# Softmax attention's denominators: ones as the stationary operand, and VectorE's 32x32 transposes in place of TensorE's

## What is computed

```python
sc = jnp.einsum("bqgrd,bkgd->bgrqk", qi, k).astype(jnp.float32) * scale
p = jax.nn.softmax(sc, axis=-1).astype(v.dtype)
return jnp.einsum("bgrqk,bkgd->bqgrd", p, v)
```

## Time and profile before

| | us |
|---|---|
| median of three runs | 1561.52 |
| profiled execution, device time | 1560.5 |
| its span | 1558.7 |
| TensorE busy | 1528.3 (98%) |
| VectorE busy | 1139.1 (73%) |
| ScalarE busy | 834.7 (54%) |
| GpSimd busy | 907.3 (58%) |

### The profile page before, as it was taken

The page is one execution under the profiler, slowest core; times in us unless marked ns, Lnnn a source line. Parts: engine busy times, 40 slices in busy tenths (PEclk is TensorE's granted clock), DMA queues, the critical chain, the costliest instruction groups (busy, mean ns, idle before and its releaser), DMA issues.

```text
span 1558.7 us, 23051 instructions
## 1 busy us (share of the span) xinstructions
PE 1528.3 (98%) x7975; PEld 1235.0 (79%) x7975; DVE 1139.1 (73%) x1590; ACT 834.7 (54%) x1552; POOL 907.3 (58%) x644
## 2 busy tenths in 40 slices
PE   7999999999999999999999999999999999999998
PEld 4778888888878766687777888888888888888887
DVE  4799888888739888488459878877768895567542
ACT  4775765766633587423344444444458665454442
POOL 0556765766655876556846767776753467532314
PEclk9999999999999999999999999999999999999999
DMA  8434434434332300276622333333422334322212
GB/s 328 133 122 129 128 108 130 131 107 129 115 94 70 81 28 1 83 239 249 214 67 83 96 92 103 108 109 109 113 83 81 95 102 122 94 62 69 68 41 82
DMA packets 77485, 171.34 MB, mean 110 GB/s; under 512 B 8321, under 2 KB 10753, under 8 KB 73921
## 3 DMA queue, kind: packets, MB, share of 16 engines
q1 hardware_dynamic: 70064, 133.09, 28.7%
q10 hardware_dynamic: 7312, 36.83, 6.7%
HBM read 167.67 MB, written 2.23 MB: 109 GB/s over the span
## 4 chain that ended last, share of the span: by engine, by line
PE 64%; DVE 13%; issue 8%; POOL 6%; DMA 2%; ACT 2%; ACTq 0%; DVEq 0%; POOLq 0%; SPq 0%
PE bank L1401 8%; PE bank L1403 7%; PE bank L1402 7%; PE bank L1419 7%; PE bank L1422 7%; PE bank L1420 7%; POOL w_lo L716 6%; PE bank L1864 4%; DMA w_raw<-ws 2%; PE bank L1866 2%; DVE ada_acc L2155 2%; PE bank L1757 2%; DVE rstd L2454 2%; PE bank L2021 1%; PE bank L1695 1%
## 5 line engine op out<-in xcount | busy, mean ns | idle before, releaser
L716 POOL TENSOR_TENSOR w_lo<-w_raw,w_hi 128x512 fp32r<-128x512 f32 x440 | 644.8, 1489 | 403.2 <-ACT w_hi L775 402.8
L775 ACT ACTIVATE w_hi<-w_raw 128x512 fp32r<-128x512 f32 x444 | 260.4, 624 | 124.0 <-DMA w_raw<-ws 104.2
L1401 PE MATMUL bank<-a_hi_and_lo,w_hi 128*128 128x512 f32 (+1 forms) x800 | 315.8, 395 | 2.4 <-ACT gates_early L840 1.2
L1403 PE MATMUL bank<-a_hi_and_lo,w_lo 128*128 128x512 f32 (+1 forms) x800 | 308.7, 386 | 0.0
L1402 PE MATMUL bank<-a_hi_and_lo,w_hi 128*128 128x512 f32 (+1 forms) x800 | 308.3, 385 | 0.0
L1419 PE MATMUL bank<-b_hi,w_hi 128*128 128x512 f32 x536 | 210.2, 392 | 2.6 <-ACT tmp L1119 1.4
L1422 PE MATMUL bank<-b_lo,w_hi 128*128 128x512 f32 x536 | 209.2, 390 | 0.0
L1420 PE MATMUL bank<-b_hi,w_lo 128*128 128x512 f32 x536 | 209.0, 390 | 0.0
L1401 PEld LDWEIGHTS bank<-a_hi_and_lo,w_hi 128*128 128x128 f32 x800 | 150.4, 188 | 36.6 <-issue 4.4
L1402 PEld LDWEIGHTS bank<-a_hi_and_lo,w_hi 128*128 128x128 f32 x800 | 150.5, 188 | 30.8 <-issue 1.9
L1403 PEld LDWEIGHTS bank<-a_hi_and_lo,w_lo 128*128 128x128 f32 x800 | 150.3, 188 | 30.8
(11 more groups left out here) (447 smaller groups left out, 3183.2 us busy)
## 6 DMA issues: line engine op xcount, KB each, us to landing
w_raw<-ws SPq DMA_DIRECT2D x457, 256.0 KB, 2.7
cs_rows<-cs_scratch ACTq DMA_DIRECT2D x16, 1024.0 KB, 5.2
ada_piece<-ada ACTq DMA_DIRECT2D x16, 1024.0 KB, 5.3
ada_piece<-ada SPq DMA_DIRECT2D x8, 1024.0 KB, 17.6
x_stream<-x SPq DMA_DIRECT2D x2, 1024.0 KB, 8.5
x_stream<-x ACTq DMA_DIRECT2D x1, 2048.0 KB, 7.8
out<-x_stream SPq DMA_DIRECT2D x4, 256.0 KB, 3.3
out<-x_stream SPq DMA_DIRECT2D x8, 128.0 KB, 1.8
```

The costliest lines, as they stand in the source:

```text
L716: nc.gpsimd.tensor_tensor(wlo[b][:, :], full[:, :], r32(whi[b][:, :]), ALU.subtract)\
L775: A(whi[n % RING][:, :], full[:, :], ACT.Copy).then_inc(hi_done, 1)
L1401: mm(out, lh, rh, start=first, stop=False)
L1403: return mm(out, ll, rh, start=False, stop=last)
```

## The change

`take_sums` now makes two matmuls for a pair instead of eight: 64 columns of ones are the stationary operand and the whole `sq[hh]` the moving one, and head 0's sums land on partitions 0 to 63, head 1's on 64 to 127, each repeated over 64 partitions, with the queries in the free dimension. Both stand behind `row_of_max`. VectorE transposes this bank in 32x32 blocks to t[4], inverts one column of each block (16 columns), and transposes these, each repeated 32 times, back to t[5], which has the layout that `scale_pair` multiplies with. `sums_to_columns` stands behind the first maximum of an odd head, `invert_sums` behind the second. `spread_inverse` and `keep_inverse` of ScalarE and `turn_inverse` of TensorE are gone.

```diff
@@ -579,8 +580,8 @@
 
         slab_used, FILLED = fills, N_KV
-        chunks_added, sums_taken, sums_inverted, inverse_turned = exp_masked, st_done, rec_done, xt_done
-        inverse_kept, q_high, inverse_spread = x_kept, e_ready, xs_sc
+        chunks_added, sums_taken = exp_masked, st_done
+        q_high, sums_copied = e_ready, xs_sc
         ADDED_AT, SCANNED = 2 * PAIRS, PAIRS
 
...
@@ -993,19 +994,6 @@
 
-            def spread_inverse(u):
-                act.wait_ge(sums_inverted, SCANNED + u + 1)
-                if u >= 2:
-                    act.wait_ge(o_ev, u - 1)
-                else:
-                    act.wait_ge(yz_ready, PAIRS)
-                A(t[4 + u % 2][:, :].rearrange("p (i d) -> p i d", d=HD),
-                  inv_sum[:, :, None].broadcast_to([P, 2 * NCH, HD]), ACT.Copy).then_inc(inverse_spread, 1)
-
-            def keep_inverse(u):
-                act.wait_ge(inverse_turned, SCANNED + u + 1)
-                A(t[4 + u % 2][:, :], SUMS[:, :], ACT.Copy).then_inc(inverse_kept, 1)
-
             def query_high(h):
...
@@ -1758,25 +1740,16 @@
                 ins.then_inc(pv_done, 1)
 
-            def take_sums(u, hh):
-                pe.wait_ge(chunks_added, ADDED_AT + (NCH - 1) * (2 * u + hh + 1))
+            def take_sums(u):
+                pe.wait_ge(chunks_added, ADDED_AT + (NCH - 1) * (2 * u + 2))
                 if u:
-                    pe.wait_ge(inverse_kept, SCANNED + u)
+                    pe.wait_ge(sums_copied, SCANNED + u)
                 else:
                     pe.wait_ge(qk_std, len(QK))
-                for i in range(NCH):
-                    ins = mm(SUMS[:, (2 * i + hh) * HD:(2 * i + hh + 1) * HD], sq[hh][:, i * P:(i + 1) * P], ones[:, 0:HD], start=True, stop=True)
-                ins.then_inc(sums_taken, 1)
-
-            def last_sums():
                 for hh in range(2):
-                    take_sums(QT - 1, hh)
-
-            def turn_inverse(u):
-                pe.wait_ge(inverse_spread, SCANNED + u + 1)
-                for i in range(NCH):
-                    ins = nc.tensor.transpose(SUMS[:, i * P:(i + 1) * P], t[4 + u % 2][:, i * P:(i + 1) * P], ident)
-                ins.then_inc(inverse_turned, 1)
+                    rows_of = slice(hh * HD, (hh + 1) * HD)
+                    ins = mm(SUMS[rows_of, :], ones[:, rows_of], sq[hh][:, :], start=True, stop=True)
+                ins.then_inc(sums_taken, 2)
 
             def middle_of(n):
...
@@ -1819,26 +1792,20 @@
                 chunks_of(h, 0, NCH)
                 if h % 2 == 0:
-                    take_sums(u - 1, 0)
                     row_of_max(h + 1)
-                    take_sums(u - 1, 1)
+                    take_sums(u - 1)
                     continue
                 if u == 0:
...
                 for c in range(NCH):
                     values(u, c)
-                    if c == 1:
-                        if h + 1 < N_Q:
-                            row_of_max(h + 1)
-                        if u:
-                            turn_inverse(u - 1)
+                    if c == 1 and h + 1 < N_Q:
+                        row_of_max(h + 1)
             for m in range(KT):
                 if m >= N_EARLY:
                     feature_tile(("ga", m), in_a, in_a_lo)
-                feature_tile(("gs", m), in_a, in_a_lo, mid=None if m else last_sums)
-                if m == 0:
-                    turn_inverse(QT - 1)
+                feature_tile(("gs", m), in_a, in_a_lo, mid=None if m else lambda: take_sums(QT - 1))
                 feature_tile(("wa", m), in_b, in_b_lo, (rdyB, PAIRS))
                 if m == KT - 3:
...
@@ -2501,16 +2468,23 @@
                 V.tensor_tensor(qL[b][0:HD, :], qF[own, u, :], r32(qHH[b][own, :]), ALU.subtract).then_inc(q_ready, 1)
 
+            def columns_of(wide):
+                return wide[:, :].rearrange("p (b c) -> p b c", c=SQUARE)
+
+            def sums_to_columns(u):
+                ve.wait_ge(sums_taken, SCANNED + 2 * (u + 1))
+                V.transpose(t[4][:, :], SUMS[:, :]).then_inc(sums_copied, 1)
+
             def invert_sums(u):
-                ve.wait_ge(sums_taken, SCANNED + 2 * (u + 1))
-                if u:
-                    ve.wait_ge(inverse_spread, SCANNED + u)
-                V.reciprocal(inv_sum, SUMS[:, :].rearrange("p (i d) -> p i d", d=HD)[:, :, 0]).then_inc(sums_inverted, 1)
+                ve.wait_ge(sums_copied, SCANNED + u + 1)
+                v(V.reciprocal(inv_sum, columns_of(t[4])[:, :, 0]))
+                v.settle()
+                v(V.transpose(columns_of(t[5]), inv_sum[:, :, None].broadcast_to([P, SEQ // SQUARE, SQUARE])))
 
             def scale_pair(u):
                 ve.wait_ge(pv_done, NCH * (u + 1))
-                ve.wait_ge(inverse_kept, SCANNED + u + 1)
-                V.tensor_tensor(OQ[u % 2][:, :], OQ[u % 2][:, :], t[4 + u % 2][:, :], ALU.mult).then_inc(o_ev, 1)
+                v.settle()
+                V.tensor_tensor(OQ[u % 2][:, :], OQ[u % 2][:, :], t[5][:, :], ALU.mult).then_inc(o_ev, 1)
 
             def split_pair(u):
...
@@ -2541,10 +2515,15 @@
             for h in range(N_Q):
-                if h + 1 < N_Q:
-                    for i in range(NCH):
+                u = h // 2
+                turned = h % 2 and u
+                for i in range(NCH):
+                    if h + 1 < N_Q:
                         max_of(h + 1, i)
-                u = h // 2
+                    if turned and i == 0:
+                        sums_to_columns(u - 1)
+                    if turned and i == 1:
+                        invert_sums(u - 1)
                 if h in (1, 3):
...
@@ -2563,9 +2542,8 @@
                     if u >= 2:
                         split_pair(u - 2)
-                    if u:
-                        invert_sums(u - 1)
             split_pair(QT - 2)
+            sums_to_columns(QT - 1)
             invert_sums(QT - 1)
             scale_pair(QT - 1)
```

More of the change, by code:

```diff
@@ L282 @@
     SUM_AT[_name] = _s
+SQUARE = 32
 ADA_W = 2 * D_MODEL
@@ L405, in build @@
         mx = [maxima[:, 0:NCH], maxima[:, NCH:2 * NCH]]
-        inv_sum = small[:, 312:320]
+        inv_sum = cwh[:, 128:144]
         with Arena():
@@ L1038, in _ @@
                     continue
-                if u:
-                    spread_inverse(u - 1)
-                else:
+                if u == 0:
                     query_high(3)
@@ L1046, in _ @@
                     max_row(h + 1)
-                if u:
-                    keep_inverse(u - 1)
                 if h + 4 < N_Q:
@@ L1051, in _ @@
             round_pair(QT - 2)
-            spread_inverse(QT - 1)
-            keep_inverse(QT - 1)
             round_pair(QT - 1)
```

## The result

The changed kernel takes 1567.78 us, the median of six runs (1564.13 to 1570.84), the one before 1561.80 on the same chips: a ratio of 1.0039, 95% interval 1.0028 to 1.0049. That is 6.0 us slower, where 3.7 were forecast; the value lies in the range that was stated, 1559.3 to 1570.5. The profiled execution is the fastest of the six, 1564.13 us with a span of 1562.3, 3.6 us over the span before.

What follows compares the result with a forecast made beforehand. TensorE, busy 98% of the span, was taken as the bound, with waits for VectorE's maxima opening in its queue. Losses of 5.45 us less 1.75 at the end gave +3.7 us: median 1565.2 us, range 1559.3 to 1570.5.

Steps and rivals of the forecast that it cites:

- rival 2: VectorE's transposes are cheap or hidden in its slack: -2 to +3 us, 1559.5 to 1564.6; chance 33%.
- Prices: Costs per pair: new sums 1.0 us on TensorE; on VectorE transposes 0.69 and 0.74, reciprocal 0.26.
- Rivals 3 and 4: Transposes at half rate, about 1.1 us each: 1570, 12%; sums not side by side: 1572, 3%.
- Even head, +0.25: Even head to next odd: TensorE idles some 0.9 us before the row of maxima, sums follow it; 0.25 us longer.
- Plain odd head, +0.1: Odd to even head, heads 11 and 13: maxima 0.5 us later eat the 0.44 us saved; 0.1 us longer.
- Heads 3 and 7, +0.5 with the even part: VectorE reaches the even head's maxima 1.6 us later, past its 1.14 us idle; +0.5 us each.
- the even part: The step from an even head to the next odd one, forecast 0.25 us longer, included in each pair's sum.
- Head 5, +1.8: Pair with a query tile's rotation on VectorE: 1.6 us fully on the path, 1.8 with the even part.
- head 9, +1.5: Pair with a query tile's rotation: loss as in head 5, less some 0.35 us from leaving GpSimd's adds; 1.5 us.
- it bounds the pair already, and the 1.6 us go fully onto the path: Heads 5 and 9: VectorE has no idle time before the next maxima, so its later arrival counts in full, 1.6 us.
- nobody waits: GpSimd gets its buffer about 1.1 us later, but its adds still end before the next sums; no cost.
- The end, -1.75: Last pair has no maxima, so TensorE's savings on sums and transposes count: 1.75 us shorter.

Runs made afterwards that it cites:

- E6: Kernel before the change, with only the order changed: the even head's row of maxima first, then all eight sum matmuls; ratio 1.0039.
- E2: Changed kernel with both VectorE transposes and the reciprocal moved behind the odd head's fourth maximum; ratio to the kernel before 1.0038.
- E4: Changed kernel without VectorE's transposes and reciprocal, so without the division by the sums; ratio to the kernel before 0.9992.
- E5: Kernel before the change, with two unused 32x32 transposes added on VectorE in each odd head from head 3 on; ratio 1.0015.
- E8: Changed kernel with unused matmuls filling TensorE's idle times in heads 6 and 10, eight and four in each; ratio to the kernel before 1.0016.
- E9: Changed kernel, first transpose at even head's end, reciprocal and second behind odd head's fourth maximum, sums cut by queries around the row of maxima; ratio 0.9990.
- E10: E9 with both parts of the sums ahead of the row of maxima in heads 4 and 8; 1556.46 us, ratio to the kernel before 0.9971.
- E3: Changed kernel with sums ahead of the row of maxima and both transposes and reciprocal behind the odd head's fourth maximum; ratio 1.0014.

## Why the prediction was right, and where it was not

The sign and the range hold, and so does the mechanism of the even heads. Part of the agreement is luck: the terms that were in the sum came to 2.0 us and not 3.7, which by itself is the outcome of rival 2 (partly hidden transposes, -2 to +3 us), and a term that was left out, the clock, made up for it. Point by point:

- *Prices.* Transposes of 0.71 us and sums of 1.0 us side by side: right. Rivals 3 and 4 fall. Nearest to the transposes was indeed the shuffle (0.72 to 0.77 us). The Trainium skill's 0.31 us for 128x128 in bf16 (VectorE: DVE Perf Modes, "The three transpose paths") can't be scaled by four here: 512 columns of float32 take 0.71 us here, 2.3 times as much.
- *Even head, +0.25.* Measured +0.25; 0.78 us idle where 0.9 was said. E6 shows the mechanism by itself.
- *Plain odd head, +0.1.* Measured -0.04. The row of maxima stands at 5.26 us after the head's start (632.59 - 627.33), where 5.41 was worked out and 4.86 is the value before: the 0.40 us by which it is later eat nearly all of the 0.43 us that the missing transposes give behind it. It is earlier than forecast because transposes and maxima follow each other every 0.61 to 0.63 us and not every 0.66 to 0.71. E2 and E4 show that 0.36 and 0.34 us are to be had there, and E5 that the same work put into the kernel before costs 0.36. A plain pair takes 12.67 us, against 12.46 before and 12.8 forecast.
- *Heads 3 and 7, +0.5 with the even part.* Measured +0.18. VectorE was to reach the even head's maxima 1.6 us later, past its 1.14 us of idle time. By the timelines of head 3 it ends `scale_pair`, the last work ahead of them, 8.21 us after the head's start instead of 7.39, so 0.82 us later and within the idle time: the low part of the queries, which waits for a GpSimd add, takes 0.91 us instead of 1.27.
- *Head 5, +1.8, and head 9, +1.5.* Measured +1.05, and +1.52 without the clock (E8). The step that failed is "it bounds the pair already, and the 1.6 us go fully onto the path". They don't: the rotation's first step waits for GpSimd's adds, and VectorE's extra work fits into that wait (E5: nothing in head 5). And the step on GpSimd, that it gets its buffer 1.1 us later and "nobody waits", failed the other way. It does start 1.1 us later (0.22 us after head 5's start, 0.89 before it in the kernel before), and nobody waits for the sums; but the add that VectorE waits for now ends 5.61 us after the head's start instead of 4.83. In the changed kernel's head 5 (570.87) the first step of the rotation ends at 6.16 us, not 5.37: 0.79 later, and with the even part's 0.25 that is the 1.05 measured. GpSimd's add ends at 576.48, again 0.55 us ahead of it. Two errors of opposite sign; the second fits E4's head 9, E9 and E10.

```profile
575.77 1.26 DVE L2416 TENSOR_TENSOR tmp<-tmp 128x512 f32<-128x512 f32 x1
577.07 1.68 DVE L2450 TENSOR_TENSOR q_full<-tmp,rstd 128x512 f32<-128x512 f32 x1
...
575.18 1.30 POOL L689 TENSOR_TENSOR sq<-probs_odd 128x512 f32<-128x512 f32 x1
576.91 2.99 POOL L693 TENSOR_TENSOR sq<-sq,probs_odd 128x512 f32<-128x512 f32 x2 [0.43 <-POOL sq L689]
```

  Head 9's 1.5 is right by luck. The prediction had the rotation move out from beside GpSimd's adds and get 0.35 us back. In the trace its first step is beside the sixth add in both kernels and takes 1.65 us instead of 1.16. That add ends 606.91 - 597.73 = 9.18 us after the head's start instead of 603.99 - 596.10 = 7.89, partly because it starts later and partly because it is longer. The step ends 1.29 us later, and with the even part that is about the 1.52. Before and after, head 9:

```profile
601.03 2.96 POOL L692 TENSOR_TENSOR sq<-sq,q_full 128x512 f32<-128x512 f32 x2
603.38 1.16 DVE L2449 TENSOR_TENSOR tmp<-tmp 128x512 f32<-128x512 f32 x1
...
603.47 3.44 POOL L693 TENSOR_TENSOR sq<-sq,q_full 128x512 f32<-128x512 f32 x2
605.81 1.65 DVE L2416 TENSOR_TENSOR tmp<-tmp 128x512 f32<-128x512 f32 x1
```

- *The end, -1.75.* Measured -1.62.
- *The clock*, missing from the sum. It costs 15.63 - 14.55 = 1.08 us in the pair of head 9 and 8.75 - 7.46 = 1.29 in head 11, 2.4 us in the profiled execution. The five others have no trace; their clocks are 0.992 to 0.995 against its 0.996 and they are 2.6 to 6.7 us longer, so it probably costs more there. Without it the sum would have been 2.0 us measured (E8) against 3.7 forecast; with it the profiled execution is 3.6 over and the median 6.0. So the median lies 2.3 us over the forecast because of a term that was left out, while the terms that were in it came to 1.7 us less.

That the medians differ by more than the profiled executions goes with the clocks of the runs. Which heads the clock falls in there isn't known, nor that it falls in the loop alone: E8, which only adds matmuls that nobody uses, is the evidence that most of it does. Of the 4.39 us by the timeline the span shows 3.6; matched matmul by matmul, the difference shrinks in small steps between about 730 and 935 us, for a reason that isn't known.

## What to carry to other kernels

Saved work on the busiest engine is worth what its next wait leaves of it: look at which instruction stands ahead of a wait and fills it, before moving or removing it. A later release of a buffer is a later start of its next user, and where that user shares something with a third engine, the time at which it starts is a price of its own; here the places of the sums and of VectorE's turns in their queues, not what they cost, decided between 1.0039 and 0.9971. And TensorE, when it idles for one or two microseconds, may pay twice, once for the wait and once at the lower clock.

## What the runs showed of the hardware

- VectorE's operations on two SBUF tiles wait for GpSimd's add to end (0.68 us when one began 0.09 us before the add's end, 1.65 us when it began 1.1 us before it, both ending 0.54 to 0.59 us behind the add). In the attention loops of all twelve traces, all 95 such operations of the rotation and of the queries' low parts that began more than 0.1 us after an add began ended 0.54 to 0.61 us behind that add's end. The Trainium skill (SBUF — State Buffer, "SBUF: two separate sides") says that a VectorE operation with two SBUF inputs and a GpSimd operation that reads SBUF contend for a pair of ports that is "an exclusive lock, not a bandwidth split"; the traces agree. The transposes, on one tile in SBUF or in PSUM, took 0.66 to 0.72 us whatever GpSimd did.
- In the loop TensorE's granted clock fell to its lower level after or within idle times of 1.62 and 0.79 us (the changed kernel), 1.59 and 0.78 and once more 1.61 (E2), 2.00 (E3) and 1.70 us (E9); not after 1.21 and 0.78 us (the changed kernel, head 6), 1.46 us (E3, head 10), 1.47 (E9, head 6) or single ones of 0.78. Eight and four matmuls whose results nobody uses kept it up (E8).
- A float32 transpose of 128x512 in 32x32 blocks takes 0.71 us from PSUM and, with its input repeated from 16 columns, from SBUF.
